# Scores placed inside a unit, a reordered VectorE queue, and half of a layer norm moved to GpSimd

## The reference

```
h      = RMSNorm(x)
P      = h @ W_in                  # one projection, columns shared by all branches
A      = B * conv3(C * xa)         # short causal convolution, 512 channels
Bm     = gelu(u) * (tril(W_s) @ LayerNorm(gelu(v)) + b)     # chunks of 128 tokens, 4 groups
Cm     = stick-breaking attention  # 8 heads x 64, q and k RMS-normed per head
merged = sum_i sigmoid(gate_i) * (branch_i @ W_branch_out[i])
x      = x + merged @ W_o
x      = x + (silu(g) * u2) @ W_down,   g, u2 = RMSNorm(x) @ W_gate_up
```

## Time and profile before

| | |
|---|---|
| median of 3 runs | 1646.99 us (1646.91 to 1647.17) |
| the profiled execution | 1646.85 us, span 1645.1 us |
| PE busy | 1637.0 us, 100% of the span |
| DVE busy | 969.2 us, 59% |
| ACT busy | 783.1 us, 48% |
| POOL busy | 50.8 us, 3% |
| granted TensorE clock, mean | 1.0 |

### The profile page before, as it was taken

One profiled execution on the slowest core, in us unless ns is written; L12 is line 12 of the kernel. 1 busy time (PEld: TensorE's weight loads), 2 busy tenths in 40 slices (PEclk: granted clock), 3 DMA queues, 4 the chain that ended last, 5 costly groups with the idle time before them and its releaser, 6 DMA issues.

```text
span 1645.1 us, 20945 instructions
## 1 busy us (share of the span) xinstructions
PE 1637.0 (100%) x7394; PEld 1360.0 (83%) x7394; DVE 969.2 (59%) x1302; ACT 783.1 (48%) x1113; POOL 50.8 (3%) x49
## 2 busy tenths in 40 slices
PE   9999999999999999999999999999999999999999
PEld 7888888888888888888888888888888888888887
DVE  6898887554554434434648988875455444344344
ACT  7788886333343223223457788763334432232231
POOL 1000000000110000000120000000001100000000
PEclk9999999999999999999999999999999999999999
DMA  5222222223323233232332222223233232322323
GB/s 194 95 71 77 77 86 74 97 89 102 102 91 101 94 99 98 94 103 89 124 120 90 77 77 77 78 77 98 93 102 102 90 102 90 102 92 100 96 95 128
DMA packets 46860, 158.15 MB, mean 96 GB/s; under 512 B 5456, under 2 KB 5712, under 8 KB 46800
## 3 DMA queue, kind: packets, MB, share of 16 engines
q1 hardware_dynamic: 46656, 157.34, 29.1%
q10 hardware_dynamic: 144, 0.03, 0.0%
HBM read 155.26 MB, written 2.10 MB: 96 GB/s over the span
## 4 chain that ended last, share of the span: by engine, by line
PE 88%; DVE 7%; ACT 3%; DVEq 1%; ACTq 1%; issue 1%
PE bank L461 26%; PE bank L462 26%; PE bank L465 26%; PE z L489 2%; PE z L563 1%; PE bank L489 1%; PE z L461 1%; PE z L465 1%; PE z L462 1%; DVE w_lo L1179 1%; DVE s_lo L1212 1%; PE misc L586 0%; PE misc L583 0%; DVE t_s L1207 0%; PE z L552 0%
## 5 line engine op out<-in xcount | busy, mean ns | idle before, releaser
L461 PE MATMUL bank<-xg_hi,w_hi 128*128 128x512 f32 x1472 | 574.5, 390 | 0.0
L462 PE MATMUL bank<-xg_lo,w_hi 128*128 128x512 f32 x1472 | 573.4, 390 | 0.0
L789 ACT ACTIVATE w_hi<-raw 128x1024 fp32r<-128x1024 f32 (+1 forms) x294 | 302.2, 1033 | 472.6 <-DMA raw<-in_w_units 472.2
L1179 DVE TENSOR_TENSOR w_lo<-raw,w_hi 128x1024 fp32r<-128x1024 f32 (+1 forms) x294 | 357.1, 1218 | 39.4 <-ACT w_hi L789 22.4
L465 PE MATMUL bank<-xg_hi,w_lo 128*128 128x512 f32 x1472 | 364.1, 389 | 0.0
L465 PEld LDWEIGHTS bank<-xg_hi,w_lo 128*128 128x128 f32 x1472 | 276.2, 188 | 57.2
L462 PEld LDWEIGHTS bank<-xg_lo,w_hi 128*128 128x128 f32 x1472 | 276.5, 188 | 56.7
L461 PEld LDWEIGHTS bank<-xg_hi,w_hi 128*128 128x128 f32 x1472 | 276.4, 188 | 56.8
L1184 DVE TENSOR_TENSOR S<-bank,rstd 128x512 f32<-128x512 f32 x152 | 104.9, 690 | 255.2 <-PE bank L465 253.6
L461 PE MATMUL bank<-mid_hi,w_hi 128*128 128x512 f32 x474 | 184.7, 390 | 0.0
L462 PE MATMUL bank<-mid_lo,w_hi 128*128 128x512 f32 x474 | 184.4, 389 | 0.0
(11 more groups left out here) (204 smaller groups left out, 1708.9 us busy)
## 6 DMA issues: line engine op xcount, KB each, us to landing
raw<-in_w_units SPq DMA_DIRECT2D x278, 512.0 KB, 3.3
raw<-in_w_units SPq DMA_DIRECT2D x20, 256.0 KB, 2.6
xT<-in_x SPq DMA_DIRECT2D x8, 256.0 KB, 6.6
out_x<-xT SPq DMA_DIRECT2D x7, 256.0 KB, 4.0
ln_g<-in_sgu_ln_g SPq DMA_DIRECT2D x2, 256.0 KB, 5.0
ln_b<-in_sgu_ln_b SPq DMA_DIRECT2D x2, 256.0 KB, 5.2
sgu_bias<-in_sgu_b SPq DMA_DIRECT2D x2, 256.0 KB, 5.7
sw_raw<-in_sgu_w SPq DMA_DIRECT2D x2, 256.0 KB, 5.8
```

The costliest lines, as they stand in the source:

```text
L461: mm(dst[:, :], wh[:, k0 + k, :], his[k], start=(k % per == 0), stop=False)
L462: mm(dst[:, :], wh[:, k0 + k, :], los[k], start=False, stop=False)
L789: af(w_hi[at.slot(c)][:, 0:kc, :], raw[at.slot(c)][:, 0:kc, :], ACT.Copy).then_inc(hi_done, 1)
L1179: tt(w[:, 0:kc, :], r[:, 0:kc, :], h[:, 0:kc, :].bitcast(F32), ALU.subtract).then_inc(lo_done, 1)
```

## The change

- WARM becomes 10, and the memset of its tile (L1281) becomes VectorE's first instruction, before ten semaphore increments.
- TensorE: the scores of the next pair's first head run between the 16 and the 8 matmuls of unit 7, not behind them.
- VectorE, in pairs 0 to 2: unit 6 is scaled before `mixed` and split 9, and `causal` stands before `with_u`.
- Layer norm blocks 2 and 3 are computed on GpSimd, in place in `v_tok`, by three instructions each with a drain behind every one, once `ln_rstd` is ready. Their formula is ((v - mean) * rstd) * g + b, each factor in its own step.
- ScalarE rounds them before pair 0, between the logarithms and the half copy of the first head; VectorE takes both remainders in pair 0 before split 3. The calls inside pair 0 are gone.

```diff
-WARM = 8
+WARM = 10
+        def ln_block(n):
+            return (S0[:, :], S1[:, :], v_tok[:, 2, :], v_tok[:, 3, :])[n].rearrange("p (g c) -> p g c", g=KC)
@@ GpSimd
+            def late_norm(n):
+                e = v_tok[:, n, :]
+                nc.gpsimd.tensor_scalar(e, e, ln_mv[:, n, 0:1], ln_rstd[:, n:n + 1], ALU.subtract, ALU.mult)
+                pool.drain()
+                nc.gpsimd.tensor_tensor(e, e, ln_g[:, :], ALU.mult)
+                pool.drain()
+                nc.gpsimd.tensor_tensor(e, e, ln_b[:, :], ALU.add).then_inc(ln_late, 1)
+                pool.drain()
...
                 last.then_inc(q_zero, 1)
                 pool.drain()
+                pool.wait_ge(ln_in, l * 48 + 48)
+                pool.wait_ge(ln_scaled, l + 1)
+                for n in (2, 3):
+                    late_norm(n)
@@ TensorE
-                    unit(at, 7, xh, xl)
-                    scores(h3 + 6, pairs + 1, 0)
+                    unit(at, 7, xh, xl, between=lambda: scores(h3 + 6, pairs + 1, 0))
@@ ScalarE
-                act.wait_ge(ln_pre, l * NT + n + 1)
+                if n < 2:
+                    act.wait_ge(ln_pre, l * 2 + n + 1)
+                else:
+                    act.wait_ge(ln_late, l * 2 + n - 1)
...
                 softplus_logs(l * 24)
+                ln_round(l, 2)
+                ln_round(l, 3)
                 fold_halves(l * 24)
@@ VectorE
+            nc.vector.memset(N0[:, 0:P], -1.0).then_inc(warm_in, 1)
             dve.sem_inc(unit_done, RAW)
...
-            nc.vector.memset(N0[:, 0:P], -1.0).then_inc(warm_in, 1)
...
+                dve.sem_inc(ln_scaled, 1)
                 dve.wait_ge(ln_in, l * 48 + 48)
                 layer_norm(0)
                 layer_norm(1)
...
                         scaled(at, 0, gates[:, KC, :])
-                        layer_norm(2)
                         square_lo(l * 8 + 2)
+                        layer_norm_lo(2)
+                        layer_norm_lo(3)
...
-                    mixed(m0 + M_MIX, j1)
-                    split_lo(at, 9)
-
                     scaled(at, 6, S2[:, :])
                     dve.drain()
                     dve.sem_inc(u_raw, 1)
+                    mixed(m0 + M_MIX, j1)
+                    split_lo(at, 9)
+
                     attention_lo(h3 + 3)
+                    causal(h3 + 6)
                     with_u(pairs)
                     ya_rest()
                     scaled(at, 7, flat(gates))
                     split_lo(at, 10)
-                    causal(h3 + 6)
```

More of the change, by code:

```diff
@@ L255, in build @@
         ln_chain = sem("ln_chain")
+        ln_scaled = sem("ln_scaled")
         ln_pre = sem("ln_pre")
+        ln_late = sem("ln_late")
         ln_hi = sem("ln_hi")
@@ L885, in ln_round @@
             def ln_round(l, n):
-                act.wait_ge(ln_pre, l * NT + n + 1)
-                af(yb_hi[:, :, n * P:(n + 1) * P], (S0, S1)[n % 2][:, :].rearrange("p (g c) -> p g c", g=KC),
-                   ACT.Copy).then_inc(ln_hi, 1)
+                if n < 2:
+                    act.wait_ge(ln_pre, l * 2 + n + 1)
+                else:
+                    act.wait_ge(ln_late, l * 2 + n - 1)
+                af(yb_hi[:, :, n * P:(n + 1) * P], ln_block(n), ACT.Copy).then_inc(ln_hi, 1)
             act.dma_start(par[:, :], params[0]).then_inc(par_in, 16)
@@ L1009, in pair @@
                         head_square(heads + 3, QT)
-                    if j == 0:
-                        ln_round(l, 2)
                     split_hi(at, 3)
@@ L1048, in pair @@
                     act.wait_ge(qk_nrm, heads + 4)
-                    if j == 0:
-                        ln_round(l, 3)
                     yc_half(m0 + M_E0)
@@ L1341, in layer_norm @@
                 def layer_norm(n):
-                    e = (S0, S1)[n % 2]
-                    if n >= 2:
-                        dve.drain()
+                    e = (S0, S1)[n]
                     stt(e[:, :], v_tok[:, n, :], ln_mv[:, n, 0:1], ln_g[:, :], ALU.subtract, ALU.mult)
@@ L1351, in layer_norm_lo @@
                     dve.wait_ge(ln_hi, l * 4 + n + 1)
-                    tt(yb_lo[:, :, n * P:(n + 1) * P], (S0, S1)[n % 2][:, :].rearrange("p (g c) -> p g c", g=KC),
+                    tt(yb_lo[:, :, n * P:(n + 1) * P], ln_block(n),
                        yb_hi[:, :, n * P:(n + 1) * P].bitcast(F32), ALU.subtract).then_inc(ln_ok, 1)
@@ L1521, in pair @@
                     attention_lo(h3)
-                    if j == 0:
-                        layer_norm_lo(2)
                     nch = l * CHAINS + (j * 2 + 3)
@@ L1528, in pair @@
                     causal(h3 + 3)
-                    if j == 0:
-                        layer_norm(3)
                     head_norm(nch + 1, KT, par[:, R_GK:R_GK + 1])
@@ L1534, in pair @@
                     yc_add(heads, 0)
-                    if j == 0:
-                        layer_norm_lo(3)
                     fold_sums(heads + 1)
```

## The result

The changed kernel is slower. Its median is 1653.42 us (1651.32 to 1654.98; one execution of 2045.54 at a mean clock of 0.753 is left out), against 1647.12 (1646.86 to 1647.8) for the kernel before: a ratio of 1.0034, interval 1.0023 to 1.0045. The profiled execution took 1651.42 us, where the prediction had 1651.1 for it and 1651.2 for the median. So the profiled execution is hit within 0.3 us, and the median is 2.2 above.

The account below looks back on a forecast made before the run. TensorE was taken as the bound, busy 1637 of 1645.1 us. On the profiled 1646.85, 2 x (3.65 - 1.44) - 0.2 = +4.2 gave 1651.1, median 1651.2; range 1642.4 to 1654.2, likeliest case 1649.3 to 1653.9.

Parts of the forecast that it names:

- The mechanism: After ln_rstd, GpSimd's six operations fall one by one between VectorE's seven two-SBUF-input STTs, delaying them 4.85 us in all.
- Rival A: At the STTs after ln_rstd: they do not wait for GpSimd, its work hides; 1642.7 us, chance 0.15.
- Rival B: Three GpSimd operations fall ahead of L1258, the others later: delay about 2.3, stall 1.1 us; 1646.0 us, chance 0.09.
- Stall at the scores: TensorE before the scores (L551): k_rest ends at 65.83, not 60.98, so a stall of 3.65 us per layer.
- my 0.60: GpSimd's tensor_scalar, for which no row exists: taken as 0.60 us, near the cast's 0.47.
- the seven STTs: VectorE's L1346 to L1258 after ln_rstd: 1.3 to 1.9 us each instead of 0.75, as a sign.
- Pairs: Stalls before mix in pair 0 and cumulate of pair 1: 1.44 us won per layer, 0.60 left of 2.04.
- lag of 1.20: VectorE and ScalarE come out of the scores' stall 1.20 us later against TensorE, staying on the chain through pair 0.
- Pair 2: Reordering's effect in pairs 1 and 2: counted as 0, with 0.1 us per pair as bound.
- The reordering: Scores in mid unit 7, minimum and unit scaling earlier: by itself gains nothing, within 0.1 us.
- Warm-up: Start of kernel: earlier memset and ten warm matmuls remove part of the slow start; 0.2 us won, bounds 0 and 0.42.
- the fall: Rival: TensorE's clock falls in the 3.65 us wait at the scores, losing 2.2 us per layer; 1655.7 us, chance 0.07.

Follow-up runs that it names:

- the memsets: Changed kernel with GpSimd's three operations on each of blocks 2 and 3 replaced by six memsets, their layer norm left out: 1642.42 us, ratio 0.997.
- the filled kernel: Changed kernel plus 14 extra 512-column matmuls on TensorE before the first scores of each layer, results overwritten: 1650.77 us, ratio 1.002.
- the kernel with block 2 early: Against the 1642.41 us kernel: GpSimd starts block 2 at ln_rstd again, only block 3 behind k_rest: 1646.36 us, ratio 0.9995.
- the best version: Changed kernel with GpSimd's norm started behind k_rest, ScalarE's two roundings behind the folded sums' rounding, with_u ahead of the minimum: 1642.41 us, ratio 0.9969.
- the first attempt at a later start: Changed kernel with GpSimd starting its layer norm when k_rest is done, not at ln_rstd, roundings unmoved: 1647.12 us, ratio 0.9998.

## Why the prediction was right, and where its steps were off

- **The mechanism held.** Where GpSimd's instructions that read SBUF met VectorE's with two SBUF inputs, one delayed the other. Experiments: without the GpSimd part no stall at the scores; with non-reading GpSimd work none; with three instructions early 1.2; with six 3.3; with none early 0. Rival A (work hides, 1642.7) rested on an STT never being seen to wait; L1208 at 1.78 us ends that. Its number is what the kernel gives once the collision is removed (1642.42 with the memsets). Rival B (three operations ahead of L1258, 1646.0) fell too: four of the six began before L1277 (L1258 before) ended, and the other two met `k_rest`.
- **Stall at the scores: 3.30 per layer for 3.65**, just below the 3.4 to 4.7 that the prediction named as its sign (3.1 in the view of waits). The two-input operations came out as forecast, 1.16, 1.15, 1.13 and 1.11 behind the end of what they overlapped, for 1.15. The tensor_scalar was not: it ends 1.95 behind the overlapped STT's end both times (53.83 to 55.78, 59.90 to 61.85), more than the upper bound of 1.15 from the nearest rows, and yet delays the STT issued during it by only 0.34 and 0.33, less than the 0.37 I took. So it does not hold the way for as long as it runs: the STT at 54.94 ran beside the first and w_lo (L1198, 61.01, 1.21) beside the second, both at their usual length. The later one blocking for the whole instruction, which the prediction took as its rule, does not hold for this operation; the measurement decides. That my 0.60 gave nearly its delay is luck. Since it took longer, the last two GpSimd operations met `k_rest` and not the STTs. So of the seven STTs that were to take 1.3 to 1.9 us only two did (1.78 and 1.62), and `k_rest` took 1.75 more, which the prediction did not have. The total hardly changed (k_rest ends at 65.57, forecast 65.83), since `k_rest` is on the same chain as the STTs. The estimate by the figure of the Trainium skill (GPSIMD Engine Reference, "Performance versus the Vector engine"), 4.0, was further off; the operation's 1.95 us is over twice the 769 ns that the page has as its best case.
- **Pairs: 3.6 won for 2.9.** The stall before `mix` went (0.35 in each layer). Of the one before `cumulate` of pair 1 (the rows are below) 0.20 is left in layer 0 and none in layer 1, where I had 0.60 each. The two engines' lag of 1.20 was there, but in layer 0 they made up 0.4 more of it than my walk allowed. In layer 1 the slow clock helped: at full clock, in the filled kernel, 0.31 is left there. Counted in that kernel, the pairs win 3.0 (2 x 0.35 before `mix`, 1.46 and 1.37 before `cumulate` of pair 1, less 0.38 and 0.11 before that of pair 2), close to the 2.9.

Timeline of the changed kernel before `cumulate` of pairs 1 and 2, to be held against the earlier trace rows:

```profile
135.54 1.98 PE L485 MATMUL bank<-xg_hi,w_lo 128*128 128x512 f32 x8
...
136.45 0.95 DVE L1249 TENSOR_TENSOR fold_hl<-fold,fold_hl 64x768 fp32r<-64x768 f32 x1
...
137.55 0.47 PE L583 MATMUL z<-s_hi,neg_tri 128*128 128x512 f32 x1
...
190.91 0.95 DVE L1249 TENSOR_TENSOR fold_hl<-fold,fold_hl 64x768 fp32r<-64x768 f32 x1
...
192.01 0.47 PE L583 MATMUL z<-s_hi,neg_tri 128*128 128x512 f32 x1 [0.29 <-DVE fold_hl L1249]
```

- **Pair 2 was mis-sized.** I counted 0 with 0.1 as bound; the wait grew from 0.11 to 0.45 in layer 0. It appears with the GpSimd part alone, so the reordering isn't the cause. In layer 1 the clock's fall hides it; the filled kernel has 0.17 there for 0.07 before. That the lag of pair 0 travels on, once TensorE no longer stands still before pair 1, is argued and not shown.
- **The reordering brings nothing**, as forecast ("by itself gains nothing"): 1647.26 without the GpSimd part, and 1642.52 against 1642.41 with the scores on either side. In ScalarE's queue in pair 0 of the changed kernel Abs follows the table load (124.59 + 1.28, Abs at 125.89) and no longer waits for the minimum (ended 123.13): the earlier minimum only took the place of `with_u`, for which the table load waits.
- **Warm-up: 0.1 lost for 0.2 won.** The 1.26 of the first three matmuls became 1.10, but they began 0.12 later (5.73): the ten warm matmuls ended at 5.75, not before the weights were ready at about 5.5 as I had assumed. Its sign can't be told from the runs.
- **The clock is where the median went.** I gave the fall 0.07 and 2.2 us per layer; it happened in every execution but by varying amounts, 1.6 us in the profiled one. Ruling it out from a standstill of 1.69 was the weak step: twice that length was outside of what the trace had shown. The profiled execution matched so well because it was among the least affected, and because two other deviations of 0.7 us each, a shorter stall at the scores and more won in the pairs, made up for most of the clock's 1.6. The second of them was largely the clock's own doing, as said above. That this execution lies within 0.3 us of the forecast is luck; without the fall it would be the filled kernel's 1650.63, 0.5 below the forecast.

**What stays open.** Why the clock falls behind one of two equal stalls and how far; the 0.34 of pair 2; the 0.4 us of the kernel with block 2 early; why the changed kernel's median is 2 us above that of its GpSimd part alone, when that kernel too has executions at 1653.4 to 1654.1; and the 0.7 us that the best version gains beyond the stalls.

## What to carry to other kernels

Before work goes to an idle engine, look at what the receiving engine's neighbour does at the very moment it would start: here 1.2 us of slack on the critical chain met six instructions, and the same instructions one step later (behind `k_rest`) put no wait before the scores. Then ask what consumes the moved result and what is queued behind that consumer, since the first attempt at a later start lost all it had won to two roundings in ScalarE's queue. And cost a new standstill of TensorE twice, once for its length and once for the clock behind it; if it can't be avoided, filler matmuls take the second part away.

## What the runs showed of the hardware that was not expected

- GpSimd's tensor_scalar over 128x512 with two operations and scalars from SBUF takes 1.95 us beyond the STT that it overlaps, but delays the next STT by only 0.33 to 0.34; its tensor_tensor of the same size takes 1.11 to 1.16 and delays by 0.93 to 1.10.
- GpSimd's memset of 128x512 takes 0.53 us and delays nothing.
- Stalls of TensorE of 1.2 to 1.7 us left the clock at 1.0 in every run; with stalls of 3.3 us every run had a lower mean clock (0.996 to 0.999 in 13 executions of two kernels, leaving out the one at 0.753), and with the same time filled by 14 matmuls none of 11 had.
- A slow stretch that put TensorE 1.6 us behind made the profiled execution only 0.8 us longer than the filled kernel's: later stalls of TensorE shrank, by 0.31 and 0.17 us before two of the `cumulate`s.
